# A two-block decoder on one core: the set-up stage joined with the first projections

## What is computed

```python
def rms_norm(x, g):
    xf = x.astype(jnp.float32)
    y = xf * lax.rsqrt(jnp.mean(xf * xf, axis=-1, keepdims=True) + RMS_EPS)
    return (y * g.astype(jnp.float32)).astype(x.dtype)
...
    proj = xn @ w_comb
    c_b, c_c, c_x = jnp.split(proj[..., :OFF_SB], 3, axis=-1)
    q, k, v = jnp.split(proj[..., OFF_SB:OFF_GATE], 3, axis=-1)
    y_rwkv, v_first = rwkv7_time_mix(proj[..., OFF_RWKV:], mu, w0, w_lora, a0, a_lora, g_lora, ...)
```

## Time and profile before

| | |
|---|---|
| median of 3 executions | 2240.03 us (2237.8 to 2240.34) |
| the profiled execution | 2237.44 us, of which the span of the records is 2235.7 us |
| TensorE busy | 2079.4 us, 93% of the span, 11888 matmuls |
| VectorE, ScalarE, GpSimd busy | 1120.9 us (50%), 782.4 us (35%), 152.0 us (7%) |
| mean granted clock of TensorE | 0.959 of full speed (2.4 GHz) |
| transfers | 173.54 MB, mean 78 GB/s |

### The profile page before, as it was taken

One profiled execution on the slowest core, in us unless ns is written; L12 is line 12 of the kernel. 1 busy time (PEld: TensorE's weight loads), 2 busy tenths in 40 slices (PEclk: granted clock), 3 DMA queues, 4 the chain that ended last, 5 costly groups with the idle time before them and its releaser, 6 DMA issues. The chain is left out here.

```text
span 2235.7 us, 29732 instructions
## 1 busy us (share of the span) xinstructions
PE 2079.4 (93%) x11888; PEld 1649.9 (74%) x11888; DVE 1120.9 (50%) x1714; ACT 782.4 (35%) x1270; POOL 152.0 (7%) x187
## 2 busy tenths in 40 slices
PE   6999775998999999999999989989899899999997
PEld 5888424875887887888888868876566678888886
DVE  4653566437444454567775334314666664433433
ACT  3112433223223343444443222233455544422421
POOL 0000412532000000000000010000000000000000
PEclk9999687999999999999999999978999999999998
DMA  4233100001332241122233423211110122232222
GB/s 152 95 102 96 32 1 1 3 3 63 100 100 91 92 146 64 57 94 94 95 102 103 163 87 108 94 38 29 38 37 31 42 92 93 94 101 97 94 95 84
DMA packets 47853, 173.54 MB, mean 78 GB/s; under 512 B 5144, under 2 KB 7448, under 8 KB 47488
## 3 DMA queue, kind: packets, MB, share of 16 engines
q1 hardware_dynamic: 45440, 162.99, 22.0%
q0 software_dynamic: 1728, 8.23, 1.1%
q10 hardware_dynamic: 576, 0.84, 0.1%
HBM read 169.90 MB, written 2.13 MB: 77 GB/s over the span
## 5 line engine op out<-in xcount | busy, mean ns | idle before, releaser
L207 DVE TENSOR_TENSOR weights_lo<-weights_raw,weights_hi 128x1024 fp32r<-128x1024 f32 (+2 forms) x288 | 363.5, 1262 | 791.2 <-ACT weights_hi L199 791.1
L199 ACT ACTIVATE weights_hi<-weights_raw 128x1024 fp32r<-128x1024 f32 (+2 forms) x288 | 313.5, 1089 | 868.5 <-PE end_ps L232 245.7
L230 PE MATMUL sp_ps<-arena_parts,weights_hi 128*128 128x512 f32 x720 | 283.6, 394 | 3.0 <-DVE arena_parts L291 2.5
L232 PE MATMUL sp_ps<-arena_parts,weights_lo 128*128 128x512 f32 x720 | 281.6, 391 | 0.0
L231 PE MATMUL sp_ps<-arena_parts,weights_hi 128*128 128x512 f32 x720 | 281.5, 391 | 0.0
L230 PE MATMUL end_ps<-arena_parts,weights_hi 128*128 128x512 f32 x576 | 224.8, 390 | 2.2 <-DVE arena_parts L2872 1.7
L232 PE MATMUL end_ps<-arena_parts,weights_lo 128*128 128x512 f32 x576 | 224.1, 389 | 0.0
L231 PE MATMUL end_ps<-arena_parts,weights_hi 128*128 128x512 f32 x576 | 224.1, 389 | 0.0
L230 PE MATMUL fr_ps<-arena_parts,weights_hi 128*128 128x512 f32 (+1 forms) x480 | 183.7, 383 | 15.0 <-DVE arena_parts L293 8.4
L231 PE MATMUL fr_ps<-arena_parts,weights_hi 128*128 128x512 f32 (+1 forms) x480 | 181.8, 379 | 0.0
L232 PE MATMUL fr_ps<-arena_parts,weights_lo 128*128 128x512 f32 (+1 forms) x480 | 181.5, 378 | 0.0
(11 more groups left out here) (382 smaller groups left out, 3178.1 us busy)
## 6 DMA issues: line engine op xcount, KB each, us to landing
weights_raw<-w_up SPq DMA_DIRECT2D x44, 512.0 KB, 3.4
weights_raw<-w_proj SPq DMA_DIRECT2D x38, 512.0 KB, 3.5
weights_raw<-w_gates SPq DMA_DIRECT2D x32, 576.0 KB, 3.7
weights_raw<-w_ca SPq DMA_DIRECT2D x32, 512.0 KB, 3.4
weights_raw<-w_down SPq DMA_DIRECT2D x16, 704.0 KB, 4.1
weights_raw<-w_in SPq DMA_DIRECT2D x22, 512.0 KB, 3.4
weights_raw<-w_logits SPq DMA_DIRECT2D x16, 512.0 KB, 3.4
weights_raw<-w_ff1a SPq DMA_DIRECT2D x16, 512.0 KB, 3.4
```

Of the source, the lines that this page charges most:

```text
L199: act.activation(self.w_hi[:, g % 2, 0:cols], self.raw[:, g % 2, 0:cols], ACT.Copy).then_inc(self.hi_ready, 1)
L207: dve.tensor_tensor(self.w_lo[:, g % 2, 0:cols], self.raw[:, g % 2, 0:cols], self.w_hi[:, g % 2, 0:cols].bitcast(F32), ALU.subtract).then_ ...
L230: pe.matmul(out, left[0], right[0], start=start, stop=False)
L232: return pe.matmul(out, left[1], right[0], start=False, stop=stop)
```

## The change

The set-up stage is gone. Its work is in `proj_stage`, in one block, in another order:

- `load_weights` counts from the first group that its call loads, so that group 0 and group 1 can be loaded by separate calls.
- SyncE issues x piece 0, weight group 0, the other three pieces, group 1, the first 256 columns of the constants (`ident` and `ones`), the other constants, the two small matrices (which ScalarE issued before), and then group 2 and on.
- TensorE multiplies group 0 tile by tile as the parts of x become ready (`lowered`), then group 1, and then the sums (behind waits for the constants and the adds), group 2, the spreading, and 31 groups.
- ScalarE first takes one root of a number that VectorE has set (`warm`), then splits x and groups 0 and 1; the eight squares come behind the second group. VectorE likewise.

```diff
--- before.py
+++ after.py
@@ load_weights
-        if g0 == 0:
-            done = 2
+        if g0 < 2:
+            done = min(2 - g0, n)
@@ setup_stage: removed, see the listing above
-def setup_stage(core):
...
@@ proj_stage
+                x_piece(0)
+                core.load_weights(sp, "proj", 0, 1)
+                for n in range(1, pieces):
+                    x_piece(n)
+                core.load_weights(sp, "proj", 1, 2)
+                sp.dma_start(core.const[:, 0:first_cols], core.dram["const"][:, 0:first_cols]).then_inc(first_in, 16)
+                sp.dma_start(core.const[:, first_cols:], core.dram["const"][:, first_cols:]).then_inc(const_in, 16)
+                sp.dma_start(core.arena[:, 53, :], core.dram["wa_lora"]).then_inc(wa_in, 16)
+                sp.dma_start(core.arena[:, 54, :], core.dram["g_lora_t"]).then_inc(g_in, 16)
+                core.preloaded["proj"] = 2
                 core.stream(sp, "proj")
 
             @block.tensor
             def _(pe):
                 x = lambda k: core.pair(XN_HI, XN_LO, k)
+                pe_gemm(core, pe, 1, KD, x, ps, lowered=split.lowered)
+                pe_gemm(core, pe, 1, KD, x, ps)
+                pe.wait_ge(first_in, 16)
+                pe.wait_ge(added, KD - 2)
                 scale.sums(pe)
-                pe_gemm(core, pe, 2, KD, x, ps)
+                pe_gemm(core, pe, 1, KD, x, ps)
                 scale.spread_out(pe)
-                pe_gemm(core, pe, 12, KD, x, ps)
-                pe_gemm(core, pe, 12, KD, x, ps)
-                pe_gemm(core, pe, 8, KD, x, ps)
+                pe_gemm(core, pe, 31, KD, x, ps)
                 pe.wait_ge(scale.ready, 1)
                 pe_by_token(core, pe, 4, T, x, NT, lambda i, half: ps_v[:, i, :])
 
             @block.scalar
             def _(act):
+                act.dma_start(core.vec[:], core.dram["vec"]).then_inc(vec_in, 16)
+                act.wait_ge(warm_in, 1)
+                act.activation(core.small[:, 79:80], core.small[:, 78:79], ACT.Sqrt).then_inc(warm, 1)
+                act.wait_ge(vec_in, 16)
+                for k in range(KD):
+                    if k % per == 0:
+                        act.wait_ge(x_in[k // per], 16)
+                    split.hi(act, k)
+                    if k == 1:
+                        core.split_hi(act, g0)
+                core.split_hi(act, g0 + 1)
+                for k in range(KD):
+                    act.activation(square[:, k, :], core.h[:, k, :], ACT.Square).then_inc(squared, 1)
+                core.split_hi(act, g0 + 2)
+                core.split_hi(act, g0 + 3)
                 scale.root(act)
-                for n in range(38):
+                scale.keep(act)
+                for n in range(2, 38):
                     core.split_hi(act, g0 + n + 2)
-                    if n == 0:
-                        scale.keep(act)
...
             @block.vector
             def _(dve):
...
+                dve.memset(core.small[:, 78:79], 1.0).then_inc(warm_in, 1)
+                dve.sem_inc(core.banks_free, 4)
+                for k in range(KD):
+                    split.lo(dve, k)
+                    if k == 1:
+                        core.split_lo(dve, g0)
+                core.split_lo(dve, g0 + 1)
+                for k in range(2, KD):
+                    add(k)
+                core.split_lo(dve, g0 + 2)
                 scale.mean(dve)
+                core.split_lo(dve, g0 + 3)
+                dve.wait_ge(first_in, 16)
                 scale.invert(dve)
                 for n in range(38):
-                    core.split_lo(dve, g0 + n + 2)
                     if n == 0:
                         dve.wait_ge(scale.ready, 1)
+                        take(0)
+                        core.split_lo(dve, g0 + 4)
+                        continue
+                    if n > 2:
+                        core.split_lo(dve, g0 + n + 2)
```

More of the change, by code:

```diff
@@ L440, in proj_stage @@
     steps = core.sem("proj_steps")
+    pieces = 4
+    per = KD // pieces
+    square = core.arena[:, 40:48, :]
+    warm, warm_in = core.sem("proj_warm"), core.sem("proj_warm_in")
+    vec_in, first_in, const_in = core.sem("vec_in"), core.sem("const_first_in"), core.sem("const_in")
+    wa_in, g_in = core.sem("wa_lora_in"), core.sem("g_lora_in")
+    x_in = [core.sem(f"x_in{n}") for n in range(pieces)]
+    split = h_split(core, "mix_in", "norm_mix")
+    squared, added = core.sem("mix_in_squared"), core.sem("mix_in_added")
+    first_cols = 2 * P
     with ExitStack() as ctx:
@@ L449, in _, with x_piece @@
             def _(sp):
+                def x_piece(n):
+                    sp.dma_start(core.h[:, n * per:(n + 1) * per, :], core.dram["x_t"][:, n * per:(n + 1) * per, :]).then_inc(x_in[n], 16)
+                x_piece(0)
[8 more added lines that the diff above has]
+                core.preloaded["proj"] = 2
                 core.stream(sp, "proj")
@@ L473, in _ @@
                     act.activation(value[:, i, :], ps_v[:, i, :], ACT.Copy, scale=scale.inverse[:, i:i + 1])
+                act.wait_ge(warm, 1)
+                act.wait_ge(const_in, 16)
+                act.wait_ge(wa_in, 16)
+                act.wait_ge(g_in, 16)
             @block.vector
@@ L518, in convolve, with add @@
                     chained(dve.tensor_tensor(core.arena[:, j, :], y, b, ALU.mult))
+                def add(k):
+                    dve.wait_ge(squared, k + 1)
+                    if k >= 4:
+                        dve.wait_ge(added, k - 3)
+                    dve.tensor_tensor(square[:, k % 2, :], square[:, k % 2, :], square[:, k, :], ALU.add).then_inc(added, 1)
+                dve.memset(core.small[:, 78:79], 1.0).then_inc(warm_in, 1)
[8 more added lines that the diff above has]
+                core.split_lo(dve, g0 + 2)
                 scale.mean(dve)
+                core.split_lo(dve, g0 + 3)
+                dve.wait_ge(first_in, 16)
                 scale.invert(dve)
                 for n in range(38):
-                    core.split_lo(dve, g0 + n + 2)
                     if n == 0:
                         dve.wait_ge(scale.ready, 1)
+                        take(0)
[3 more added lines that the diff above has]
+                        core.split_lo(dve, g0 + n + 2)
                     if n < 34:
@@ L3045 @@
 STAGES = [
-    setup_stage,
     proj_stage,
```

## The result

The changed kernel takes 2225.06 us in the median of 4 executions (2223.04 to 2225.89), the one before 2239.57 (2237.8 to 2240.34): a ratio of 0.994, with a 95% interval of 0.9925 to 0.9955. Two later comparisons gave 0.9944 (0.9925 to 0.9963) and 0.9933 (0.9920 to 0.9946). It is faster: by 14.4 to 15.3 us between the medians, with intervals from 8 to 18 us.

What follows compares the result with a forecast made beforehand. TensorE, idle for the first 20.3 us, was taken to bound the projections; an earlier start and faster sums bring group 4 11.8 to 12.9 us forward, middle 12.4, from 2240.03 to a stated 2227.5 us, range 2224.5 to 2231.5.

Steps and rivals of the forecast that it cites:

- The start of TensorE: First product of group 0 in the projections: starts at 9.0 us, right if 8.7 to 9.5.
- the landing of group 0's weights: Transfers at the start: second in the new queue order, group 0's weights land at 6.5 us.
- The sums: 16 one-column token-sum matmuls, now at the fast clock behind group 1: 1.80 us instead of 3.41.
- Groups 0 and 1: First 48 projection matmuls: 12.63 us if the clock rises after eight, 13.8 after 14 slow ones.
- Rival C: Clock stays at 1.2 GHz through groups 0 and 1, starved for tiles: 8.0 us lost, 2235.5; chance 0.11.
- What waits behind: Halves of groups 2 to 5, diagonal and scale: each ready some 2 us or more before TensorE wants it.
- The sum: Start of group 4 in the projections: 11.8 to 12.9 us earlier than 48.13, middle 12.4.
- "one every 0.63 us" of the upper parts: ScalarE in the old set-up: upper parts of x said to come one every 0.63 us, alternating with squares.
- rival B: Group 0's weights land at 9.0 instead of 6.5, TensorE starts at 11.5: 2.5 us lost, 2230; chance 0.12.

Runs made afterwards that it cites:

- sums_first: Changed kernel with the token sums and their two waits put ahead of group 0 again; 2235.93 us.
- pe_warm_2: Changed kernel with 18 unneeded full-width matmuls ahead of group 0, their memset on GpSimd; 2221.17 us, ratio to the kernel before 0.9923.
- before_3: The kernel before, unchanged, run for a third trace; 2238.95 us.
- again: The changed kernel run once more, unchanged; 2224.69 us against 2239.10 for the kernel before, ratio 0.9944.
- before_2: The kernel before, unchanged, run for a second trace; 2239.84 us.
- pe_warm: Changed kernel with 18 unneeded matmuls of 512 columns on a tile of ones ahead of group 0; 2226.43 us, ratio to the kernel before 0.9932.
- again_2: The changed kernel, unchanged, run beside pe_warm_2 on the same chip; 2223.89 us against 2239.19 for the kernel before, ratio 0.9933.
- whole_x: Changed kernel with TensorE waiting for all eight tiles of x before group 0; 2226.49 us in one execution.
- more_loads: Changed kernel with 4.2 MB of spare transfers in SyncE's queue ahead of group 2's weights; 2237.97 us in one execution.
- no_early_table: Changed kernel without the early root on a constant, so tables load where first needed; 2221.87 us in one execution.

## Why the prediction was right

**The start of TensorE.** Forecast 9.0, measured 8.68, at the edge of what was to count as right (8.7 to 9.5). The term that was a little off is the landing of group 0's weights, which I had at 6.5: ScalarE could start on their upper half at 6.33, directly behind the second tile, instead of 6.55. What is left is 0.1 us in the lower half, ready at 8.63, and in the start behind it. The experiments that undo one part give its price each: 4.2 us for the tiles, 2.7 for the order and the queues of the transfers, 1.3 for the table, 1.2 for the squares. No run undoes two of them together, and I do not add them up.

**The sums.** 1.80 us instead of 3.41 at the slow spacing was forecast, 1.70 + 0.09 measured. sums_first shows both the price of their old place and that they take 3.40 there.

**Groups 0 and 1.** 12.63 to 13.8 us were forecast for the 48 matmuls; measured from the first start to that of the sums are 13.77, 12.98 and 13.53. Over all the traces of kernels that start cold, 8 to 14 starts were slow, so both ends of the term occur. The traces show no gap for a tile in group 0. Rival C is out at the slow spacing, and pe_warm_2 shows that even at the fast one the tiles come in time.

**What waits behind.** Each of the waits came where it was put: group 2's halves ready at 19.8 (19.8 forecast), group 3's at 25.6 (24.9), the diagonal at 26.4 (25.9), group 4's at 33.6 (32.9), the later ones 0.5 to 0.7 us behind the forecast, since the sums began 0.85 us behind its 21.6.

**The sum.** 11.8 to 12.9 us at group 4; measured 12.08 in the first pair, and 12.84 between the means of three traces each (48.61 and 35.76). That difference is carried on: in the first pair the next stage starts 12.09 us earlier (225.03 against 237.12), and the span is 12.7 shorter: between them lie 0.5 us in the stick-breaking stage (70.1 against 69.6), and every other stretch from stage to stage agrees within some 0.1 us. Nothing was given back.

**Slips that cost nothing.** The "one every 0.63 us" of the upper parts is the distance to the square behind each; they start 1.13 us apart (6.38 and 7.53). Two transfers of 0.5 MB stood ahead of group 0's weights in SyncE's queue before, not the three of rival B. Rival C counts its 8.0 us from 12.63, while 2227.5 holds 13.2 for the two groups; from there it is 7.4. None of them enters the sum.

**What was too small.** The medians lie 14 us apart, not 12.4. The time, 2225.06, is inside the stated range but near its lower end (2224.5); that it came so close in the first pair (2225.0 forecast, 2224.78 measured) is in part luck, since the start brought 12.08 of it and not 12.4. Of this the traces explain a part: the first pair set the start with the fewest slow matmuls (8) against one with the most (14), and at group 4 the means of three traces each are 0.4 us above my 12.4. Another 1.2 us appears in the stick-breaking stage (69.3 us in the mean of three traces against 70.5), where no instruction has changed. There TensorE is starved and its granted clock goes to and fro between its two levels (in the first trace of before 0.50 from 247 to 257 us, 1.00 from 297 to 307). The windows of that stretch in before_3 and in again (ends rounded to 0.1 us; columns: TensorE busy, granted clock, DMA share, GB/s):

```profile
237.90:308.60 70.70, 48.41 (x208) 0.67 0.02 9
```

```profile
224.30:293.10 68.80, 45.09 (x210) 0.75 0.02 8
```

Over the traces the stretch is on the whole the shorter the higher its granted clock: 70.5 to 70.8 us at 0.67 (before_2, before_3, sums_first, pe_warm), 70.1 at 0.69 (the first trace of before), 69.6 at 0.70 (the changed kernel's first trace), 69.4 at 0.73 (again_2), 68.8 at 0.75 (again), and the experiments not named here fall in line (69.6 at 0.70, 69.4 at 0.73, 69.1 and 68.9 at 0.75); whole_x falls out with 71.4 at 0.69. The moment of arrival does not order them: pe_warm and pe_warm_2 come to the stage earliest (222.7 and 222.5) and have 70.7 and 69.6, more_loads comes at 233.7 and has 68.9. So this 1.2 us goes with the clock granted in that stage; whether the change as such brings it, or these three traces were lucky, stays open.

The same holds for what lies behind. From the first matmul of the stick-breaking stage to the end, where all these kernels have the same instructions, the three traces of before took 1998.5, 2000.3 and 1999.3 us and the three of the changed kernel 1998.0, 1996.9 and 1994.3. But the eight experiments took anything from 1993.8 (no_early_table) to 2005.1 (pe_warm). The mean difference of 3.0 us between before and changed is well within that scatter. What the experiments show as the change's own is the 12.8 us at group 4; the rest of the 14 us is not shown to come from it.

**The scatter.** The result of each execution has its mean granted clock, and span goes with it. In the comparison with again, the kernel before had spans of 2235.1 and 2235.8 us at 0.959, the changed one 2221.2, 2221.7 and 2222.2; at 0.955 the one before 2243.2, 2243.8 and 2243.5, and at 0.954 the changed one 2230.0. A straight line through 49 executions (22 of before from the two later comparisons, 15 of the changed kernel, 12 with dummies), with one slope and a level for each kernel, falls 1.9 us for each 0.001 of clock. Its levels at 0.958 are 2237.7, 2223.4 and 2220.8: the change gains 14.3 us (standard error 0.4) and the dummies another 2.6 (0.5), where the traces show 1.6 to 2.6 at group 4. Laid through each of the two later comparisons alone, the line gives 13.8 and 15.5 us for the change and 1.8 and 2.8 for the dummies, so these standard errors are too small. Nor does it test the rival of pe_warm_2, that the dummies worsen the later clock: the mean clock with dummies was a little lower in both comparisons (0.9572 against 0.9575, and 0.9575 against 0.9582), and a reckoning at equal clock leaves just that out. The records of the clock leave out the start of the program (in the changed kernel's trace it reads 1.00 from 8 to 14 us, at a spacing of 0.43), so that the reckoning at equal clock does not take the slow starts out of the difference. I did not show what decides the clock of the later stages in an execution. With the dummies the kernel is the fastest of those measured, by this reading at equal clock and by pe_warm_2 against again_2; by plain medians pe_warm against again says the opposite.

## What to carry to other kernels

At the start of a program ask what the first product needs, and let only that stand in front of it, on each engine and in the transfer queue: here one tile of x and one weight group. What feeds a later step (squares, sums, constants, a table) goes behind, with its slack written beside it. Judge such an edit of a few microseconds by a fixed instruction in the trace, not by the time of single executions.

## What the runs showed of the hardware

- The cold start lasts a different number of matmuls in each execution: 8 to 14 at 0.43 us in twelve traces. The Trainium skill (TensorE: Matmul & The Clock Gate, Part 1) says that it differs from run to run; these traces agree.
- The 16 matmuls of one column that ran back to back for 3.4 us ahead of group 0 did not spare it the slow starts: 8, 11 and 12 in the kernel before, 10 in sums_first. The 18 of full width in pe_warm_2, which took 6.1 us, did, and 1.4 us of idle time behind them did not bring the slow spacing back. The two differ in length as well as in width, and no run parts the two.
- Transfers from HBM into SBUF ran at 421 GB/s from 6 to 8 us in the kernel before, and at 434 in more_loads from 20.3 to 23.7 us. The Trainium skill (DMA: Bandwidth & Descriptors, Bandwidth) says that the HBM side binds such transfers at some 358 GB/s. The Trainium skill says in the same section that this is a core's share when both cores of a pair stream, and that a core alone reached 425. Here one core was at work, and its rates agree with the second statement: 358 did not bind.
